# Pool mixer of a two-layer decoder trunk: start corrections put into the first block's band, and a separate buffer, split by GpSimd, for the next map's first weight unit

## The reference, cut to what matters

```python
def multiscale_pool_mixer(h, w_grp, b_grp, scale):      # h (1, 512, 1024), 4 groups of 256 channels
    for g, w in enumerate((2, 4, 8, 16)):
        win_sum = trailing sum of h over w positions     # by cumulative sums
        cnt = jnp.minimum(t + 1, w)                      # the first w-1 tokens have fewer terms
        outs.append(win_sum / cnt - h[group g])
    mixed = einsum("bsgc,gce->bsge", pooled, w_grp)      # one 256x256 map for each group
    return scale * (mixed + b_grp)

def conv_ffn(h, w_up, w_dw, b_dw, w_down):
    up = einsum("bsd,df->bsf", h, w_up)                  # 1024 -> 2 x 2816
    act, gate = up[..., :2816], up[..., 2816:]
    act = causal_dwconv(act, w_dw, b_dw)                 # width 3
    return einsum("bsf,fd->bsd", silu(act) * gate, w_down)
```

## Time and profile before

| quantity | value |
|---|---|
| median of three runs | 960.61 us |
| time of the profiled execution | 961.15 us |
| its span, first to last instruction | 959.3 us |
| outside the span | 1.85 us |
| PE busy | 942.9 us (98%) |
| DVE, ACT, POOL busy | 558.0, 386.8, 107.2 us |
| mean granted TensorE clock | 0.993 |

### The profile page before, as it was taken

How to read it: one execution, slowest core, us unless ns; L and a number is a source line. 1 busy time by engine, 2 the same in 40 slices (tenths; PEclk the granted TensorE clock), 3 DMA queues, 4 the chain that set the end, 5 groups by cost and what they waited for, 6 DMA issues and landing times.

```text
span 959.3 us, 11867 instructions
## 1 busy us (share of the span) xinstructions
PE 942.9 (98%) x4492; PEld 792.5 (83%) x4492; DVE 558.0 (58%) x713; ACT 386.8 (40%) x592; POOL 107.2 (11%) x71
## 2 busy tenths in 40 slices
PE   8999999999999999999999999999999999999996
PEld 6889898888888888888888898788888888888886
DVE  6899995557655565554434359666555555532333
ACT  7785695444333433332322355433334333321220
POOL 0658795000000000000000000000000000000000
PEclk9999998999999999999999999999999999999998
DMA  7220022222322222312223332223222222223212
GB/s 265 100 88 1 1 89 88 88 88 91 121 95 87 87 87 93 125 61 90 89 93 94 112 110 88 88 91 115 100 87 87 87 93 99 66 89 116 90 61 88
DMA packets 17020, 88.56 MB, mean 92 GB/s; under 512 B 2016, under 2 KB 4320, under 8 KB 9952
## 3 DMA queue, kind: packets, MB, share of 16 engines
q1 hardware_dynamic: 16416, 87.67, 26.8%
q10 hardware_dynamic: 576, 0.52, 0.2%
HBM read 86.09 MB, written 2.10 MB: 92 GB/s over the span
## 4 chain that ended last, share of the span: by engine, by line
PE 91%; DVE 5%; DMA 1%; issue 1%; ACT 1%; SPq 1%; POOL 0%; DVEq 0%
PE bank L1084 29%; PE bank L1086 28%; PE bank L1085 28%; DVE bank L819 2%; DMA w_raw<-w_pw 1%; PE bank L1146 1%; DVE out_sb L1075 1%; DVE w_lo L731 1%; PE bank L1152 0%; PE bank L1135 0%; PE bank L1136 0%; PE bank L1137 0%; PE bank L1270 0%; PE bank L1266 0%; PE bank L1267 0%
## 5 line engine op out<-in xcount | busy, mean ns | idle before, releaser
L1084 PE MATMUL bank<-h_hi,w_hi 128*128 128x512 f32 x816 | 318.8, 391 | 2.2 <-DVE w_lo L731 1.3
L1086 PE MATMUL bank<-h_hi,w_lo 128*128 128x512 f32 x816 | 317.5, 389 | 0.0
L1085 PE MATMUL bank<-h_lo,w_hi 128*128 128x512 f32 x816 | 317.5, 389 | 0.0
L439 ACT ACTIVATE w_hi<-w_raw 128x2048 fp32r<-128x2048 f32 (+2 forms) x88 | 149.2, 1695 | 212.8 <-PE bank L1086 212.8
L731 DVE TENSOR_TENSOR w_lo<-w_raw,w_hi 128x2048 fp32r<-128x2048 f32 (+2 forms) x82 | 164.4, 2005 | 101.4 <-ACT w_hi L439 100.7
L1084 PEld LDWEIGHTS bank<-h_hi,w_hi 128*128 128x128 f32 x816 | 153.2, 188 | 35.1 <-issue 1.8
L1086 PEld LDWEIGHTS bank<-h_hi,w_lo 128*128 128x128 f32 x816 | 153.2, 188 | 32.1
L1085 PEld LDWEIGHTS bank<-h_lo,w_hi 128*128 128x128 f32 x816 | 153.2, 188 | 31.9 <-issue 0.5
L1085 PE MATMUL bank<-u_lo,w_hi 128*128 128x512 f32 (+1 forms) x422 | 159.5, 378 | 0.0
L1084 PE MATMUL bank<-u_hi,w_hi 128*128 128x512 f32 (+1 forms) x374 | 141.1, 377 | 0.4 <-DVE w_lo L731 0.4
L1086 PE MATMUL bank<-u_hi,w_lo 128*128 128x512 f32 (+1 forms) x374 | 140.8, 376 | 0.0
(11 more groups left out here) (185 smaller groups left out, 928.6 us busy)
## 6 DMA issues: line engine op xcount, KB each, us to landing
w_raw<-w_up SPq DMA_DIRECT2D x44, 1024.0 KB, 4.9
w_raw<-w_down SPq DMA_DIRECT2D x32, 704.0 KB, 4.1
w_raw<-w_pw SPq DMA_DIRECT2D x11, 1024.0 KB, 4.9
x_res<-x SPq DMA_DIRECT2D x3, 512.0 KB, 7.5
out<-out_sb SPq DMA_DIRECT2D x12, 128.0 KB, 1.8
w_raw<-w_pw SPq DMA_DIRECT2D x4, 256.0 KB, 7.2
w_raw<-w_pool SPq DMA_DIRECT2D x2, 512.0 KB, 3.7
band_raw<-band SPq DMA_DIRECT2D x1, 800.0 KB, 6.1
```

The lines of the kernel that those rows point to most:

```text
L439: nc.scalar.activation(w_hi[s][:, 0:columns], w_raw[s][:, 0:columns], ACT.Copy).then_inc(w_rounded[s], 1)
L1084: M.matmul(dst, a, hi, start=start, stop=False)
L1085: M.matmul(dst, a, lo, start=False, stop=False)
L1086: return M.matmul(dst, b, hi, start=False, stop=stop)
```

## The change

- The two correction products of each tile (16 columns) are gone. A new buffer `band_first` (128 x 4 groups x 256) holds the band of block 0 with the correction added into its first 16 columns; POOL makes these 16 columns, ACT copies the other 240. The products of block 0 read it instead of `band`.
- The first up-projection unit of layer 1 has its own `up_hi` and `up_lo`, in memory of `u_lo` that is free at that time. ACT rounds it right behind the last weight rounding of layer 0, in the place where the band was rounded; POOL splits it, not DVE. PE's first unit reads these (`weights=`).
- ACT rounds the band earlier, in the last step of layer 0's down projection.
- `sum_by_token` of the mixer moves from behind group 0 to behind the first block of group 1.
- DVE does U(0) to U(3) first, then S(0), then S(1), U(4), S(2), U(5), S(3), U(6), S(4), U(7), then S(5), S(6), S(7). ACT rounds the unit of slot 1 after tile 3 instead of tile 5.
- In the next unit of slot 1, `sum_by_token` and the spreading stand before k = 4 and k = 6 instead of 5 and 7.

```diff
@@ -205,6 +205,11 @@
+        AFTER_POOL = U_HI + 2 * BLOCKS * D * 4 + KD * T * 4
+        up_hi = place("up_hi", [P, UNIT], f32r, AFTER_POOL)
+        up_lo = place("up_lo", [P, UNIT], f32r, AFTER_POOL + UNIT * 4)
+        band_first = place("band_first", [P, len(WINDOWS), 2 * P], f32r, AFTER_POOL + 2 * UNIT * 4)
+
         bank = [ctx.enter_context(nc.psum_tensor(f"bank{b}", [P, T], f32)) for b in range(8)]
...
@@ -427,6 +432,13 @@
+            pool.wait_ge(w_rounded[0], M_UP[1] + 1)
+            nc.gpsimd.tensor_tensor(up_lo[:, :], w_raw[0][:, :], as_f32(up_hi[:, :]), SUB).then_inc(w_split[0], 1)
+            plain = band[:, 0:len(WINDOWS) * BAND].rearrange("p (g c) -> p g c", g=len(WINDOWS))
+            starts = band[:, len(WINDOWS) * BAND:BAND_COLS].rearrange("p (g c) -> p g c", g=len(WINDOWS))
+            pool.wait_ge(band_rounded, 1)
+            nc.gpsimd.tensor_tensor(band_first[:, :, 0:START], as_f32(plain[:, :, P:P + START]), as_f32(starts), ADD).then_inc(first_rounded, 1)
+
         CONSTS = 8 + max(WINDOWS) - 1
@@ -654,10 +666,17 @@
+            def round_band():
+
+                act.wait_ge(band_loaded, 16)
+                nc.scalar.activation(band[:, :], band_raw[:, :], ACT.Copy).then_inc(band_rounded, 1)
+
             def down_step(layer, j, columns):
...
                 for t in range(2):
+                    if columns[t] == POOL_UNIT:
+                        round_band()
                     round_unit(0, m + 2 * j + t + 1, columns[t])
@@ -666,15 +685,18 @@
-                    act.wait_ge(band_loaded, 16)
-                    nc.scalar.activation(band[:, :], band_raw[:, :], ACT.Copy).then_inc(band_rounded, 1)
+                    act.wait_ge(raw_loaded[0], 16 * (M_UP[1] + 1))
+                    act.wait_ge(unit_done[1], M_POOL)
+                    nc.scalar.activation(up_hi[:, :], w_raw[0][:, :], ACT.Copy).then_inc(w_rounded[0], 1)
                     act.wait_ge(stat_mm, 3)
...
                     act.wait_ge(rms_ready, 3)
+                    act.wait_ge(band_rounded, 1)
                     for group in range(len(WINDOWS)):
                         if group == 3:
-                            round_unit(0, M_UP[1], UNIT)
+                            plain = band[:, 0:len(WINDOWS) * BAND].rearrange("p (g c) -> p g c", g=len(WINDOWS))
+                            nc.scalar.activation(band_first[:, :, START:2 * P], as_f32(plain[:, :, P + START:3 * P]), ACT.Copy).then_inc(first_rounded, 1)
                         for j in range(BLOCKS):
@@ -684,7 +706,7 @@
                         nc.scalar.activation(pool_sq[:, c, :], x_res[:, c, :], ACT.Square).then_inc(squared, 1)
-                        if c == 5:
+                        if c == 3:
                             round_unit(1, M_UP[1], UNIT)
@@ -1010,22 +1032,20 @@
                     clear_sums()
-                    for group in range(len(WINDOWS)):
-                        if group == 3:
-                            split_unit(0, M_UP[1], UNIT)
+                    def split_maps(group):
+
                         for j in range(BLOCKS):
...
-
                     def split_updated(c):
...
-                    dve.wait_ge(shifted, KD)
-                    for c in range(KD):
+                    def update(c):
+
                         w = WINDOWS[c // 2]
@@ -1038,9 +1058,18 @@
                         V.scalar_tensor_tensor(x_res[:, c, w - 1:T], src[:, w - 1:T], gain, x_res[:, c, w - 1:T], MUL, ADD).then_inc(x_updated, 1)
-                        if c:
-                            split_updated(c - 1)
-                    split_updated(KD - 1)
+
+                    for group in range(len(WINDOWS)):
+                        split_maps(group)
+                    dve.wait_ge(shifted, KD)
+                    for c in range(4):
+                        update(c)
+                    split_updated(0)
+                    for c in range(4, KD):
+                        split_updated(c - 3)
+                        update(c)
+                    for c in range(5, KD):
+                        split_updated(c)
@@ -1079,20 +1108,21 @@
-            def three_passes(dst, s, w_at, hi, lo, start, stop):
-                a, b = w_hi[s][:, w_at:w_at + P], w_lo[s][:, w_at:w_at + P]
+            def three_passes(dst, s, w_at, hi, lo, start, stop, weights=None):
+                w = weights or (w_hi[s], w_lo[s])
+                a, b = w[0][:, w_at:w_at + P], w[1][:, w_at:w_at + P]
                 M.matmul(dst, a, hi, start=start, stop=False)
...
-            def unit(s, m, hi, lo, before=None, at_bank=None):
+            def unit(s, m, hi, lo, before=None, at_bank=None, weights=None):
...
                     for t in range(2):
-                        last = three_passes(bank[(2 * s if at_bank is None else at_bank) + t][:, :], s, (2 * k + t) * P, hi[:, k, :], lo[:, k, :], k == 0, k == KD - 1)
+                        last = three_passes(bank[(2 * s if at_bank is None else at_bank) + t][:, :], s, (2 * k + t) * P, hi[:, k, :], lo[:, k, :], k == 0, k == KD - 1, weights)
                 last.then_inc(unit_done[s], 1)
@@ -1197,10 +1227,10 @@
-                if k == 5:
+                if k == 4:
                     pe.wait_ge(summed, (KD + 1) * 4)
                     sum_by_token(sumsq[:, :], start=True, stop=True).then_inc(stat_mm, 1)
-                if k == 7:
+                if k == 6:
                     spread(1)
@@ -1283,7 +1313,8 @@
                     wait_drained((2 * s, 2 * s + 1), DRAINED_UP[layer] + i)
-                    unit(s, M_UP[layer] + i, h_hi, h_lo, second_norm if first and layer == 1 and s == 1 else h)
+                    at_pool = first and layer == 1
+                    unit(s, M_UP[layer] + i, h_hi, h_lo, second_norm if at_pool and s == 1 else h, weights=(up_hi, up_lo) if at_pool and s == 0 else None)
                     if first and layer == 0 and s == 0:
@@ -1369,12 +1400,13 @@
                             last.then_inc(map_mm, 1)
-                        if group == 0:
-
-                            pe.wait_ge(summed, (KD + 1) * 3)
-                            sum_by_token(sumsq[:, :], start=True, stop=True).then_inc(stat_mm, 1)
+                            if (group, j) == (1, 0):
+
+                                pe.wait_ge(summed, (KD + 1) * 3)
+                                sum_by_token(sumsq[:, :], start=True, stop=True).then_inc(stat_mm, 1)
                     pe.wait_ge(band_rounded, 1)
+                    pe.wait_ge(first_rounded, 2)
                     for c in range(KD):
@@ -1391,16 +1423,13 @@
                         for j, first_out, first_col in ((0, 0, P), (2, 2 * P, P), (1, P, P), (3, 2 * P, 0)):
+                            columns = band_first[:, group, :] if j == 0 else band[:, at_band + first_col:at_band + first_col + 2 * P]
                             for n in range(2):
-                                product = M.matmul(dst[:, first_out:first_out + 2 * P], parts[2 * j + n], band[:, at_band + first_col:at_band + first_col + 2 * P],
-                                                   start=j == 0 and n == 0, stop=False, skip_group_check=True)
+                                last = M.matmul(dst[:, first_out:first_out + 2 * P], parts[2 * j + n], columns,
+                                                start=j == 0 and n == 0, stop=j == 3 and n == 1, skip_group_check=True)
                                 if c == 0 and j == 0 and n == 0:
-                                    product.then_inc(unit_done[1], 1)
-
-                        at_start = len(WINDOWS) * BAND + group * START
-                        for n in range(2):
-                            last = M.matmul(dst[:, 0:START], parts[n], band[:, at_start:at_start + START], start=False, stop=n == 1, skip_group_check=True)
+                                    last.then_inc(unit_done[1], 1)
                         last.then_inc(window_mm, 1)
```

More of the change, by code:

```diff
@@ L252, in build @@
         u_rounded, u_split = sems("u_rounded"), sems("u_split")
-        band_loaded, band_rounded, pool_vecs = sem("band_loaded"), sem("band_rounded"), sem("pool_vecs")
+        band_loaded, band_rounded, first_rounded, pool_vecs = sem("band_loaded"), sem("band_rounded"), sem("first_rounded"), sem("pool_vecs")
         shifted = sem("shifted")
```

## The result

The changed kernel takes 956.43 us (median of 6 runs, 954.72 to 957.10) against 960.61 us before. By the medians that is 4.2 us or 0.44% faster, beyond the 0.2% that count as a change. The ratio estimated from all runs, which is not a ratio of medians, is 0.9949 with a 95% interval of 0.9940 to 0.9959; the 0.9956 of the medians lies inside it. One execution of the kernel before took 5430.22 us, one of e4 took 1178.53, and one of the kernel before beside e5 to e8 took 1058.50; these three are left out of every median and ratio here. The forecast was 956.0 in a range of 955.1 to 958.0.

A forecast was written before the change was run, and what follows sets the result against it. PE, busy 98%, bounds the kernel, so only its idle time and products can go. Gains 3.65 + 1.1 - 0.1 = 4.65 us bring profiled 961.15 to 956.5; the median, 0.54 lower, gives 956.0, range 955.1 to 958.0.

The forecast's parts named there:

- next unit: After the mixer's windows, PE starts the next ConvFFN at about 580.5 instead of 584.31, a gain of 3.8 us.
- POOL done: Before window 0, POOL finishes its split and the 64 `band_first` elements at 570.5, with 2.2 us in hand.
- second step: PE's next step after the second ConvFFN unit starts at 604.5 instead of 609.13, without a wait for `act_in`.
- The sum's place: In the mixer's maps, a block of group 1 fills PE's gap before `sum_by_token`: 0.72 us gained.
- Short products and U(0): In the mixer's windows, dropped 16-column products and shorter waits, with DVE's first update 2.6 us earlier, gain 3.2 us.
- The tail: In the second unit, earlier spreading removes PE's wait for the scaled results before its next step: 1.1 us gained.
- The even points: S(5), the second unit's sums and window 7 are just in time, costing up to 0.3 us each, 0.9 in all.
- Rival 1: In the mixer's maps, POOL's split blocks DVE and the gain shrinks by 2.4 us: 958.4 us; chance 0.06.
- POOL late: Before window 0, POOL takes up to one more split of 4.63 us: 1.8 us lost, 957.8; chance 0.04.
- Rival 2: In the windows, DVE stays the bound by its new order: about 1.2 us lost, 957.2 us; chance 0.09.
- Rival 4: Behind the mixer, a later wait gives PE's early start back and the end stays: 960.3 us; chance 0.04.
- Rival 3: In ACT's queue, a late landing of the first weight unit delays everything; at 15 us, 963.2 us; chance 0.02.

The follow-up runs named there:

- e4: Changed kernel with the second unit's `sum_by_token` and spreading back before k = 5 and 7: 956.75 us, ratio to before 0.9962.
- e5: Kernel before with only the second unit's `sum_by_token` and spreading moved to before k = 4 and 6: 959.09 us, ratio to before 0.9985.
- e8: Changed kernel with POOL's split of the first up-projection unit done twice, one after the other: 958.56 us, ratio to before 0.9981.
- e6: Kernel before with only the mixer's `sum_by_token` moved behind the first block of group 1: 959.58 us, ratio to before 0.9994.
- e1: Changed kernel with the sixteen 16-column correction products back, `band_first` made but not read: 957.08 us, ratio to before 0.9964.
- e2: Changed kernel with DVE instead of POOL splitting the first up-projection unit, between the maps of groups 2 and 3: 956.47 us, ratio to before 0.9964.
- e3: Changed kernel with DVE's old order of updates and splits and ACT's rounding of slot 1 after tile 5: 956.08 us, ratio to before 0.9959.
- e7: Changed kernel with one more DVE addition of two SBUF tiles, result unread, beside POOL's split: 959.26 us, ratio to before 0.9991.
- e9: Changed kernel with S(5) ahead of U(7) on DVE: 956.08 us, ratio to before 0.9954.
- e10: Changed kernel with 16 more filler products in three places of layer 0's LayerNorm statistics: 957.28 us, ratio to before 0.9969.
- e11: Changed kernel with 16 filler products in layer 0's LayerNorm statistics and S(5) ahead of U(7) on DVE: 957.47 us, ratio to before 0.9972.

## Why the prediction was right

Step by step, from A (560.36 before and 560.15 after; the forecast's times are given 0.21 us earlier):

| step | forecast | measured |
|---|---|---|
| sum without idle time | 563.56 | 563.56 |
| window 0 | 572.47 | 572.46 |
| POOL done | 570.3 | 569.86 |
| U(0) | 574.34 | 574.33 |
| next unit | 580.3 | 580.31 |
| second unit | 591.44 | 591.57 |
| `sum_by_token` of the second unit | 596.9 | 597.05 |
| second step | 604.3 | 604.46 |
| B - A, change | -4.65 | -4.46 |

- **The sum's place** gave 0.72 us alone (e6); in company window 0 comes 0.73 us earlier from A.
- **Short products and U(0)**: the two chains were each right, and they meet at the next unit within 0.2 us (580.14 for PE alone, 580.31 with S(1)). That they are not additive is e1: 1.11 of 1.8 us.
- **DVE's relief** is worth 0.91 us, not the 2.29 us of the instruction (e2), and the order 0.74 us (e3); the forecast did not price these one by one, only their joint effect.
- **The tail**: 1.1 us forecast, 0.93 to 1.13 measured (e4, e5).
- **The even points** were real: the wait before k = 5 costs 0.21 us with its restart (587.00 to 587.34, and the next product 0.33 us later instead of 0.23), where 0.15 had been taken; the sums cost 0.15, where 0.1 had been taken. With 0.02 at the next unit these are most of the 0.19 us by which the gain fell short of the forecast. The range for this was 0.9 us.
- **POOL**: nothing taken, nothing found (4.64 us; 10 maps beside it in 4.01 us, 0.40 each). Rival 1 is wrong for this kernel since `map_lo` has one operand in PSUM; its mechanism is real (e7). Its price was 2.4 us in the forecast; in e7 PE's wait cost 2.24, and a fall of the clock behind it, which the forecast had nowhere, 1.57 more.
- **POOL late**: 1.8 us forecast, 1.61 in e8.
- **Rival 2** (DVE's chain slower than its rows) did not come: U takes 1.10 us. **Rival 4**: 350.17 and 350.14 us behind B. **Rival 3**, the late landing, didn't occur; no run made the DMA late, so its price is only argued.

The median came out 0.43 us above the forecast, while the profiled execution, 956.41, lies 0.09 below the 956.5 that the same sum gives for it. The difference is the step from the one to the other: the forecast took off 0.54 us, by which the profiled execution of the kernel before stood above its median, and that of the changed kernel stands at its median. That the profiled time fits to 0.09 us is in part luck, since 0.19 us too little in the mixer met an A that happened to be 0.21 us earlier. The spread of the changed kernel's runs is 2.4 us; what supports the forecast is B - A and the steps in the table, not the median. The lower end of the range, 955.1, was not worked out from anything; the sum's own range began at 955.4.

Two parts of the change have no run of their own: the band's rounding at its new place (548.34, with ACT idle for 2.87 us before its next rounding, so hidden there), and ACT's rounding of slot 1 after tile 3.

## What to carry to other kernels

When two engines chase each other through a stage, follow both as lists of start times to the point where the next stage waits, and take the later; the price of an instruction on one of them is only what it shifts that point by (2.28 us of split were 0.91, 1.8 us of products 1.11). The work given to the idle GpSimd was free here, with slack to its first reader and nothing beside it on VectorE that reads two SBUF operands; one such addition cost 2.2 us of waiting, and 1.6 more by the clock that fell behind the wait. Where every wait has shrunk to 0.1 us, moving an instruction only moves the wait (e9).

## What the runs showed of the hardware that was not expected

- A profile's early stretch moves everything behind it: A lies between 558.87 and 561.48 us in these profiles, of nearly the same code up to there. Two places make the difference. One is the first 20 us, where profiles drift apart by up to 1.2 us; in the changed kernel's the clock is 0.91 there, in that of the kernel before 1.00. The other is the LayerNorm stage. In layer 0 the granted clock falls to 0.50 (1.2 GHz) there, between 146 and 151 us, and is back between 152 and 157 us, at moments that differ by 3 us or more between profiles; shortly before, PE runs one-column products (from 145.66 us in the changed kernel, whose clock falls between 148 and 149). That these products bring the fall is not shown: the fillers of e10 and e11, which kept it away, stood between them. Parts of 1 us can't be read from medians of 6 to 12 runs here; a cut by two events of the same profile reads them to a few hundredths, as e10 and e11 show.
- With fillers the clock stayed at 1.00 throughout that stage and the kernel was no faster: the stage took 1.3 us more than in the changed kernel, whose clock fell.
- In e7 a wait of PE of 2.09 us was followed by a granted clock of 0.50, and the 24 products behind it took 4.45 us instead of 2.88; in e8 a wait of 2.00 us was not.
- In e7 both sides of the port lock show in a row: DVE's 0.69 us instruction took 4.32, then POOL's 0.32 us instruction took 0.76. Each ended soon after the one that it waited for, 0.55 and 0.17 us.
